# The order of three VectorE steps in the last stage of a one-core encoder block

## The chip, the cores and the metric

The kernel runs on one NeuronCore of a Trainium2 chip. The metric is the device time of one execution in microseconds (us). The times given are medians of several runs; the profile is that of one further execution.

## The reference, cut to what matters

The block is an attention mixer followed by a product-key expert layer. All the work around the change lies in the expert layer, whose experts are single neurons chosen per token. For 256 tokens of width 2048 and 16384 experts:

```python
def block_fn(args):
    tb, ib, gb = args
    u = expert_u[ib]
    a = jax.nn.gelu(jnp.einsum('thkd,td->thk', u, tb), approximate=False)
    vv = expert_v[ib]
    return jnp.einsum('thk,thkd->td', (gb * a).astype(vv.dtype), vv)
...
x = x + peer_ffn(h, peer_wq, peer_keys, peer_u, peer_v)
return rms_norm(x, norm_final_g)
```

The kernel computes the first 214 tokens densely: the products with all rows of `peer_u` (stage "u"), the gelu and the gates, and then the products with all rows of `peer_v` (stage "down"). The other 42 tokens are computed by gathering just the rows that their gates chose, three copies of 42 tokens side by side (126 partitions).

## The kernel before, in words

Each stage streams its weights in **chunks** of 128 x 1024 float32 (512 KB). To multiply in float32 accuracy, each operand is split into a high half (a rounded copy in the type fp32r) and a low half (the rest). A chunk passes through these engines:

- SP issues its load into one of four `raw` buffers (`load`, line 474). It first waits on `lo_ready`, until the low half of the chunk four earlier is made, since that is the last reader of the buffer.
- ScalarE copies `raw` to `hi` (`hi_of`, line 637) and, in the down stage, makes the high half of the chunk's activations in one of four `act_now` buffers (`act_hi_of`, line 956).
- VectorE makes the activations' low half (`act_lo_of`, line 1564; it waits for that chunk's `act_hi_of`) and the weights' low half (`lo_of`, line 1047; it waits for `hi` and, through `low_used`, until TensorE is done with the chunk two earlier, since there are two `lo` buffers).
- TensorE multiplies: eight products of `hi` with both halves of the activations (line 1962, the "highs"), and eight of `lo` with the high half (line 1966, the "lows"). Even chunks do highs and then lows, odd chunks lows and then highs. So the lows of an even chunk and of the odd one behind it stand next to each other, and TensorE needs the two `lo` tiles shortly after one another.

The down stage has 256 chunks, numbered here from 0, in two halves of 128 (output columns 0 to 1023, then 1024 to 2047). `BODY` is 4: the loops do four chunks a round, `s` is the place in the round.

Between chunks VectorE has a second job, the **row work** for the 42 gathered tokens. In chunks 2, 4, ..., 36 of the stage there is a dot product of a gathered row (`dots_at`, line 1486), then two small steps on the weights (`weights_at`), and then 43 row additions in each half (`rows_at`, lines 1599 and 1602). In the first half the additions come in nearly every second chunk, in the second half in nearly every third. GpSimd issues the gathers for this work (line 599) into three `rows` buffers; each waits for the row work that frees its buffer.

All orders are written out by hand and each engine executes its own in sequence. The VectorE function `down` is what the change touches.

Of the kernel before, what the change touches and what calls it, by code (L numbers as in the profile page):

```python
# [37 lines left out]
BODY = 4  # L38
# [93 lines left out]
HALF = CHUNKS["down"] // BODY // 2  # L132
# [128 lines left out]
def build(nc, A, out):  # L261
    with ExitStack() as ctx:
# [199 lines left out]
        def pick1(t, i):  # L462
            return flat(t[:, bass.ds(i, 1), :])
# [575 lines left out]
        def _(v):  # L1039
# [3 lines left out]
            def lo_of(cb, it, s):  # L1043

                v.wait_ge(hi_ready, it * BODY + cb + s + 1)
                v.wait_ge(low_used, it * BODY + cb + s - LOS + 1 + RAW)
                nc.vector.tensor_tensor(lo[s % LOS][:], raw[s % RAW][:], hi[s % RAW][:].bitcast(F32), ALU.subtract  # L1047
                                        ).then_inc(lo_ready, 1)
# [440 lines left out]
            def dots_at(it, s):  # L1489
                for n in dots_of(it, s):  # L1490
                    dot_of(n)
# [69 lines left out]
            def act_lo_of(it, s, j):  # L1561

                v.wait_ge(act_hi_ready, it * BODY + (s + 1))
                nc.vector.tensor_tensor(act_now[s % ACTS][:, TD:2 * TD], pick1(act, j), act_now[s % ACTS][:, 0:TD].bitcast(F32),  # L1564
                                        ALU.subtract).then_inc(act_lo_ready, 1)
# [15 lines left out]
            def weights_at(it, s):  # L1581
                if (it, s) == (WEIGHED, 1):
                    v.wait_ge(dot_done, STEPS)
                    nc.vector.tensor_tensor(w_s, dots[0:NP, 0:PICKS], dots[0:NP, PICKS:STEPS], ALU.add).then_inc(w_summed, 1)
                if (it, s) == (WEIGHED + 1, 1):
                    v.wait_ge(w_gelu, 1)
                    v.wait_ge(idx_ready, 1)
                    nc.vector.tensor_tensor(w_s, w_s, gates_s[0:NP, :], ALU.mult).then_inc(w_ready, 1)

            def rows_at(it, s, half):  # L1590
                for m in adds_of((it - HALF * half) * BODY + s, half):
                    n = half * PICKS + m
                    own = acc[0:NP, half * CW:(half + 1) * CW]
                    g = STEPS + n
                    row = rows[g % ROWS][0:NP, :]
                    v.wait_ge(row_landed[g % ROWS], 16 * (g // ROWS + 1))
                    if m == 0:
                        v.wait_ge(w_ready, 1)
                        nc.vector.tensor_scalar(own, row, w_s[:, 0:1], None, ALU.mult).then_inc(row_added, 1)
                    else:  # L1600
                        v.wait_ge(row_added, n)
                        nc.vector.scalar_tensor_tensor(out=own, in0=row, scalar=w_s[:, m:m + 1], in1=own,  # L1602
                                                       op0=ALU.mult, op1=ALU.add).then_inc(row_added, 1)

            def down(it, half, last=False):
                for s in range(BODY):
                    if not (last and s == 3):
                        if it not in (0, HALF) or s:
                            act_lo_of(it, s + 1, (it - HALF * half) * BODY + s + 1)
                        lo_of(CHUNK0["down"], it, s + 1)  # L1610
                    if half == 0:
                        dots_at(CHUNKS["u"] // BODY + it, s)
                    weights_at(it, s)
                    rows_at(it, s, half)
                    fold_squares(it, s)

            def fold_squares(it, s):

                if it == FOLDED and s in (0, 1, 2):
                    n = 4 >> s  # L1620
                    v.wait_ge(x2_sq, 2)
                    if s:
                        v.wait_ge(sq_folded, s)
                    nc.vector.tensor_tensor(sq2[:, 0:n, :], sq2[:, 0:n, :], sq2[:, n:2 * n, :], ALU.add).then_inc(sq_folded, 1)
# [16 lines left out]
            for it in range(HALF):  # L1641
                down(it, 0, last=it == HALF - 1)
# [5 lines left out]
            for it in range(HALF, 2 * HALF):  # L1648
                down(it, 1, last=it == 2 * HALF - 1)
# [500 lines left out]
```

## Time and profile before

| | |
|---|---|
| median of 3 runs | 2113.71 us (2113.15 to 2114.25) |
| profiled execution, own time | 2119.6 us |
| its span, first to last instruction | 2117.8 us |
| granted TensorE clock, mean | 0.996 of full speed |
| TensorE busy (share of the span) | 2084.9 us (98%) |
| TensorE weight loads | 1979.6 us (93%) |
| VectorE | 1618.2 us (76%) |
| ScalarE | 1178.6 us (56%) |
| GpSimd | 415.6 us (20%) |

The profiled execution took 5.9 us more than the median of the runs, and its span lies 1.8 us inside its own time. Busy time of TensorE includes pipelined matmuls whose ends are modelled, so 98% does not say that nothing was waited for; the gaps between its weight loads tell that better. The down stage begins at about 1453 us of the span and its last product starts at 2102 us.

### The profile page before, as it was taken

What the parts mean: (1) busy time and instruction counts of PE and PEld (TensorE: products, weight loads), DVE (VectorE), ACT (ScalarE), POOL (GpSimd) and SP (SyncE); (2) the same over time, 40 slices, a digit from 0 to 9 for tenths busy, and PEclk for the clock granted to TensorE, in tenths of its full rate; (3) what the DMA queues carried; (4) which work ended last, traced back from release to release, by engine and by line L of the source; (5) the groups of instructions that cost most, each with busy time, mean ns of one, the idle gap of its engine ahead of it and who ended that gap; (6) DMA issues with size and microseconds to landing.
All of it is one profiled execution on the core that took longest, in us unless ns stands there. A gap on an engine that the chain in (4) does not pass through costs nothing.

```text
span 2117.8 us, 41324 instructions
## 1 busy us (share of the span) xinstructions
PE 2084.9 (98%) x13482; PEld 1979.6 (93%) x13482; DVE 1618.2 (76%) x2678; ACT 1178.6 (56%) x2082; POOL 415.6 (20%) x306
## 2 busy tenths in 40 slices
PE   8999999999999999999999999999999999999997
PEld 6888888889989999999999999999999999999997
DVE  6555566666766986888788999888878887777776
ACT  5444455445555555555877777555554554555554
POOL 0000000000000000000766775333313321121110
PEclk9999999999999999999999999999999999999998
DMA  7655554445557456666777777999989897888883
GB/s 244 235 193 185 184 168 158 159 139 191 182 185 249 153 172 215 213 213 229 256 250 249 246 252 241 317 323 323 338 294 314 307 336 264 284 280 294 279 296 136
DMA packets 141088, 505.50 MB, mean 239 GB/s; under 512 B 16158, under 2 KB 19102, under 8 KB 140630
## 3 DMA queue, kind: packets, MB, share of 16 engines
q1 hardware_dynamic: 116072, 414.42, 57.9%
q0 software_dynamic: 24768, 90.19, 12.2%
q8 instruction: 28, 0.46, 0.1%
q14 instruction: 46, 0.38, 0.1%
q10 hardware_dynamic: 174, 0.05, 0.0%
HBM read 500.36 MB, written 4.24 MB: 238 GB/s over the span
## 4 chain that ended last, share of the span: by engine, by line
PE 89%; DVE 5%; DMA 3%; issue 2%; ACT 0%; DVEq 0%; SPq 0%; ACTq 0%
PE ps L1679 35%; PE ps L1686 19%; PE ps L1962 15%; PE ps L1966 9%; PE ps L1708 5%; DMA raw<-w_down 3%; PE ps L1944 2%; DVE lo L1047 2%; PE ps L1805 1%; PE ps L1787 1%; PE ps L1796 0%; DMA x_t<-x_t 0%; DVE acc L1602 0%; DVE score_b L1355 0%; DVE idx_now L1357 0%
## 5 line engine op out<-in xcount | busy, mean ns | idle before, releaser
L1047 DVE TENSOR_TENSOR lo<-raw,hi 128x1024 fp32r<-128x1024 f32 x760 | 925.3, 1225 | 307.4 <-PE ps L1686 200.2
L637 ACT CAST hi<-raw 128x1024 fp32r<-128x1024 f32 x760 | 791.5, 1047 | 366.0 <-DMA raw<-w_down 282.3
L1679 PE MATMUL ps<-move_u,hi 128*128 128x428 f32 x2048 | 435.2, 360 | 0.0
L1962 PE MATMUL ps<-act_now,hi 128*128 128x428 f32 x2048 | 429.2, 360 | 1.8 <-DVE x L1628 1.4
L1962 PEld LDWEIGHTS ps<-act_now,hi 128*128 128x128 f32 x2048 | 377.6, 190 | 15.3 <-DVE x L1628 2.5
L1679 PE MATMUL ps<-move,hi 128*128 128x512 f32 x1536 | 379.4, 396 | 10.1 <-ACT hi L637 10.1
L1679 PEld LDWEIGHTS ps<-move_u,hi 128*128 128x128 f32 x2048 | 371.8, 189 | 10.8
L1679 PEld LDWEIGHTS ps<-move,hi 128*128 128x128 f32 x1536 | 281.6, 189 | 63.5 <-issue 10.1
L645 ACT COPY upper<-ps 128x214 f32<-128x214 f32 (+1 forms) x224 | 78.9, 352 | 438.3 <-PE ps L1679 438.0
L1966 PEld LDWEIGHTS ps<-act_now,lo 128*128 128x128 f32 x2048 | 253.2, 192 | 8.8 <-issue 5.8
L1966 PE MATMUL ps<-act_now,lo 128*128 128x214 f32 x2048 | 255.0, 275 | 4.7 <-DVE lo L1047 3.6
L1686 PEld LDWEIGHTS ps<-move_u,lo 128*128 128x128 f32 x2048 | 248.4, 191 | 3.9 <-DVE lo L1047 1.8
L1686 PE MATMUL ps<-move_u,lo 128*128 128x214 f32 x2048 | 248.4, 274 | 1.5 <-DVE lo L1047 1.5
L1686 PEld LDWEIGHTS ps<-move,lo 128*128 128x128 f32 x1536 | 198.1, 191 | 11.2 <-DVE move L1099 1.3
L599 POOL DMA_INDIRECT rows<-u_rows,idx x86 | 114.2, 1328 | 461.4 <-ACT gates_s L878 314.2
L1686 PE MATMUL ps<-move,lo 128*128 128x256 f32 x1536 | 202.3, 284 | 1.0 <-DVE move L1272 0.9
L599 POOL DMA_INDIRECT rows<-w_down,idx x86 | 120.1, 1397 | 413.5 <-DVE acc L1602 356.8
L617 POOL TENSOR_SCALAR one_j<-iota,j_t,gate_t 128x128 f32<-128x128 f32 x107 | 170.1, 1590 | 89.2 <-PE ps L1944 85.6
L1564 DVE TENSOR_TENSOR act_now<-act,act_now 128x214 fp32r<-128x214 f32 x256 | 96.3, 376 | 57.1 <-ACT act_now L956 56.6
L1602 DVE SCALAR_TENSOR_TENSOR acc<-rows,dots,acc 126x1024 f32<-126x1024 f32 x84 | 107.4, 1279 | 1.2 <-DMA rows<-w_down,idx 1.2
L1486 DVE CUSTOM_DVE_ANT_0 rows<-rows,h_rows 126x1024 f32<-126x1024 f32 x86 | 104.7, 1218 | 0.0
L1708 PE MATMUL ps<-move,hi 128*128 128x256 f32 x512 | 97.4, 287 | 2.6 <-DVE lo L1047 2.4
(210 smaller groups left out, 1660.2 us busy)
## 6 DMA issues: line engine op xcount, KB each, us to landing
raw<-w_u SPq DMA_DIRECT2D x256, 512.0 KB, 4.3
raw<-w_down SPq DMA_DIRECT2D x256, 512.0 KB, 5.9
raw<-w_qk SPq DMA_DIRECT2D x68, 512.0 KB, 4.3
raw<-w_gate SPq DMA_DIRECT2D x64, 512.0 KB, 3.4
raw<-w_out SPq DMA_DIRECT2D x32, 512.0 KB, 3.8
raw<-w_pq SPq DMA_DIRECT2D x32, 512.0 KB, 3.3
raw<-w_v SPq DMA_DIRECT2D x28, 512.0 KB, 4.4
raw<-w_o SPq DMA_DIRECT2D x24, 512.0 KB, 3.5
```

The costliest lines, as they stand in the source:

```text
L599: nc.gpsimd.indirect_dma_start(rows[g % ROWS][:], None, lines, bass.IndirectOffsetOnAxis(ap=idx[:, n:n + 1], axis=0)).then_inc(row_landed[ ...
L617: nc.gpsimd.tensor_scalar(one_j[n % 4][:, 0, :], iota128[:], j_t[:, 2 * n:2 * n + 1], gate_t[:, 2 * n:2 * n + 1], ALU.is_equal, ALU.mult). ...
L637: nc.scalar.copy(hi[slot][:], raw[slot][:]).then_inc(hi_ready, 1)
L1047: nc.vector.tensor_tensor(lo[s % LOS][:], raw[s % RAW][:], hi[s % RAW][:].bitcast(F32), ALU.subtract).then_inc(lo_ready, 1)
L1486: nc.vector.tensor_tensor_reduce(row, row, h_rows[0:NP, c:c + CW], 1.0, 0.0, ALU.mult, ALU.add, dots[0:NP, n:n + 1]).then_inc(dot_done, 1)
L1564: nc.vector.tensor_tensor(act_now[s % ACTS][:, TD:2 * TD], pick1(act, j), act_now[s % ACTS][:, 0:TD].bitcast(F32), ALU.subtract).then_inc( ...
L1602: nc.vector.scalar_tensor_tensor(out=own, in0=row, scalar=w_s[:, m:m + 1], in1=own, op0=ALU.mult, op1=ALU.add).then_inc(row_added, 1)
L1679: ins = nc.tensor.matmul(ps[bank][:, 0:2 * w], hi[slot][:, col:col + P], m, start=begins, stop=ends)
L1686: ins = nc.tensor.matmul(ps[bank][:, 0:w], lo[lslot][:, col:col + P], m[:, 0:w], start=False, stop=False, skip_group_check=True)
L1708: ins = nc.tensor.matmul(ps[bank][:, 0:T], w[:, col:col + P], x, start=begins, stop=ends)
L1962: return nc.tensor.matmul(ps[d][:, 0:2 * TD], hi[s % RAW][:, d * P:(d + 1) * P], act_now[s % ACTS][:], start=begins, stop=ends)
L1966: return nc.tensor.matmul(ps[d][:, 0:TD], lo[s % LOS][:, d * P:(d + 1) * P], act_now[s % ACTS][:, 0:TD], start=False, stop=False, skip_gro ...
```

## The change

In each chunk's step of the down stage, `lo_of` of the next chunk now comes first, and then `act_lo_of` of the chunk after that one, where before `act_lo_of` and `lo_of` of the next chunk stood together in that order. The first two activations of each half are made ahead of the loops in both versions.

```diff
             def down(it, half, last=False):
                 for s in range(BODY):
                     if not (last and s == 3):
-                        if it not in (0, HALF) or s:
-                            act_lo_of(it, s + 1, (it - HALF * half) * BODY + s + 1)
                         lo_of(CHUNK0["down"], it, s + 1)
+                    if not (last and s >= 2):
+                        act_lo_of(it, s + 2, (it - HALF * half) * BODY + s + 2)
                     if half == 0:
                         dots_at(CHUNKS["u"] // BODY + it, s)
                     weights_at(it, s)
```

What this does to VectorE's sequence is seen in the built programs. First a place in the first half with a row addition between an even chunk (`lo0`) and the odd one behind it (`lo1`); `act_now1` is the odd chunk's activations. Before:

```order
L1564 TENSOR_TENSOR act_now0_84<-act_145,act_now0_84 128x214
L1047 TENSOR_TENSOR lo0_57<-raw0_49,hi0_53 128x1024
L1602 SCALAR_TENSOR_TENSOR acc_153<-rows2_152,dots_155,acc_153 126x1024
L1564 TENSOR_TENSOR act_now1_85<-act_145,act_now1_85 128x214
L1047 TENSOR_TENSOR lo1_58<-raw1_50,hi1_54 128x1024
```

The same place on VectorE after the change:

```order
L1564 TENSOR_TENSOR act_now0_84<-act_145,act_now0_84 128x214
L1047 TENSOR_TENSOR lo0_57<-raw0_49,hi0_53 128x1024
L1564 TENSOR_TENSOR act_now1_85<-act_145,act_now1_85 128x214
L1602 SCALAR_TENSOR_TENSOR acc_153<-rows2_152,dots_155,acc_153 126x1024
L1047 TENSOR_TENSOR lo1_58<-raw1_50,hi1_54 128x1024
```

The row addition has moved past one instruction: from ahead of the odd chunk's `act_now` to behind it, directly ahead of that chunk's `lo`. The tiles' sequence without the row work is the same. The second place is in the stage's first chunks, where the row work is a dot product (two instructions). Before, on VectorE:

```order
L1047 TENSOR_TENSOR lo0_57<-raw0_49,hi0_53 128x1024
L1486 ISA rows2_152,dots_155<-rows2_152,h_rows_147 126x1024
L1486 ISA dots_155 126x1
L1564 TENSOR_TENSOR act_now1_85<-act_145,act_now1_85 128x214
L1047 TENSOR_TENSOR lo1_58<-raw1_50,hi1_54 128x1024
```

And after the change:

```order
L1047 TENSOR_TENSOR lo0_57<-raw0_49,hi0_53 128x1024
L1564 TENSOR_TENSOR act_now1_85<-act_145,act_now1_85 128x214
L1486 ISA rows2_152,dots_155<-rows2_152,h_rows_147 126x1024
L1486 ISA dots_155 126x1
L1047 TENSOR_TENSOR lo1_58<-raw1_50,hi1_54 128x1024
```

Again the row work and `act_now` have changed places. Chunks with no row work between them show no difference, and the programs of TensorE, ScalarE, GpSimd and SP are the same in both versions.

## Rows read from the trace of the kernel before

**Rows 1.** Busy time by stretch: first half, then second half of the down stage.

```profile
core 0: us, PE busy (x) PEld busy (x) DVE busy (x) ACT busy (x) POOL busy (x), PEclk, DMA share, GB/s
1461.00:1766.00 305.00, 300.78 (x1941) 293.01 (x1941) 251.26 (x324) 158.96 (x246) 88.73 (x60) 1.00 0.90 319
1790.00:2090.00 300.00, 299.53 (x1948) 292.79 (x1946) 232.25 (x288) 164.72 (x255) 52.56 (x40) 1.00 0.82 280
```

**Rows 2.** The chain of work that ended last: start us, us, what.

```profile
1719.21 3.14 PE ps L1962 x16
1722.35 1.78 PE ps L1966 x16
1724.13 3.14 PE ps L1962 x16
```

**Rows 3.** TensorE's weight loads: lows of chunk 6, and of chunk 124.

```profile
1470.58 1.95 PEld L1966 LDWEIGHTS ps<-act_now,lo 128*128 128x128 f32 x16
...
1766.59 1.06 PEld L1966 LDWEIGHTS ps<-act_now,lo 128*128 128x128 f32 x8
```

**Rows 4.** Waits, 1461 to 1766 us: us in total, times, longest.

```profile
ACT hi L637 <- DMA raw<-w_down: 140.0, 73, 4.9
...
DVE act_now L1564 <- ACT act_now L956: 26.8, 32, 2.8
DVE lo L1047 <- PE ps L1966: 24.3, 32, 2.1
```

**Rows 5.** VectorE in order of time around chunks 56 and 57.

```profile
1591.37 1.23 DVE L1047 TENSOR_TENSOR lo<-raw,hi 128x1024 fp32r<-128x1024 f32 x1 [0.74 <-PE ps L1966]
1592.51 1.28 DVE L1602 SCALAR_TENSOR_TENSOR acc<-rows,dots,acc 126x1024 f32<-126x1024 f32 x1
1594.66 0.38 DVE L1564 TENSOR_TENSOR act_now<-act,act_now 128x214 fp32r<-128x214 f32 x1 [0.87 <-ACT act_now L956]
1594.96 1.22 DVE L1047 TENSOR_TENSOR lo<-raw,hi 128x1024 fp32r<-128x1024 f32 x1
1596.10 0.37 DVE L1564 TENSOR_TENSOR act_now<-act,act_now 128x214 fp32r<-128x214 f32 x1
```

**Rows 6.** SP's issues of the loads of chunks 57 and 61.

```profile
1585.80 0.33 SPq L474 DMA_DIRECT2D raw<-w_down  x1
...
1596.35 0.33 SPq L474 DMA_DIRECT2D raw<-w_down  x1
```

**Rows 7.** ScalarE's copies of chunks 57, 61 and 132, started by their loads' landing.

```profile
1593.31 1.05 ACT L637 CAST hi<-raw 128x1024 fp32r<-128x1024 f32 x1 [3.38 <-DMA raw<-w_down]
...
1601.76 1.05 ACT L637 CAST hi<-raw 128x1024 fp32r<-128x1024 f32 x1 [1.21 <-DMA raw<-w_down]
...
1786.19 1.05 ACT L637 CAST hi<-raw 128x1024 fp32r<-128x1024 f32 x1 [6.99 <-DMA raw<-w_down]
```

**Rows 8.** VectorE, first and last of the meetings counted in the prediction.

```profile
1468.15 1.22 DVE L1486 CUSTOM_DVE_ANT_0 rows<-rows,h_rows 126x1024 f32<-126x1024 f32 x1
...
1469.87 0.38 DVE L1564 TENSOR_TENSOR act_now<-act,act_now 128x214 fp32r<-128x214 f32 x1 [0.49 <-ACT act_now L956]
...
1759.25 1.28 DVE L1602 SCALAR_TENSOR_TENSOR acc<-rows,dots,acc 126x1024 f32<-126x1024 f32 x1
1760.71 0.38 DVE L1564 TENSOR_TENSOR act_now<-act,act_now 128x214 fp32r<-128x214 f32 x1 [0.18 <-ACT act_now L956]
```

**Rows 9.** Loads, median us to landing: 1461 to 1770 us, then 1790 to 2090 us.

```profile
raw<-w_down SPq DMA_DIRECT2D x124, 512.0 KB, 6.7
...
raw<-w_down SPq DMA_DIRECT2D x119, 512.0 KB, 5.0
```

**Rows 10.** GpSimd's gathers next to the loads of chunks 57 and 61.

```profile
1584.79 1.65 POOL L599 DMA_INDIRECT rows<-w_down,idx  x1 [3.98 <-DVE acc L1602]
...
1594.56 0.94 POOL L599 DMA_INDIRECT rows<-w_down,idx  x1 [3.41 <-DVE acc L1602]
```

**Rows 11.** The load of chunk 132, issued after a pause.

```profile
1782.79 0.33 SPq L474 DMA_DIRECT2D raw<-w_down  x1
```

**Rows 12.** VectorE in the second half: chunks 158 and 159.

```profile
1851.87 1.23 DVE L1047 TENSOR_TENSOR lo<-raw,hi 128x1024 fp32r<-128x1024 f32 x1 [0.78 <-PE ps L1966]
1855.34 0.38 DVE L1564 TENSOR_TENSOR act_now<-act,act_now 128x214 fp32r<-128x214 f32 x1 [2.24 <-ACT act_now L956]
1855.64 1.22 DVE L1047 TENSOR_TENSOR lo<-raw,hi 128x1024 fp32r<-128x1024 f32 x1
1856.78 1.28 DVE L1602 SCALAR_TENSOR_TENSOR acc<-rows,dots,acc 126x1024 f32<-126x1024 f32 x1
```

## The prediction, made before the changed kernel was run

> **What bounds the kernel now.** I looked first at busy time by stretch, since the change touches the down stage alone. In both halves TensorE's row is full (300.78 of 305 us, 299.53 of 300) at the full clock, 1.00 [rows 1]. The chain of waits then gives TensorE's own pace: from one run of 16 highs to the next is 1724.13 - 1719.21 = 4.92 us for a pair of chunks [rows 2]. The gaps between weight loads tell how near the stage is to that pace. From the lows of chunk 6 to those of chunk 124 lie 59 pairs, so 290.3 us at 4.92; the trace has 1766.59 - 1470.58 = 296.0 [rows 3]. TensorE waited 5.7 us there, 5.02 us a pair.
>
> What it waits for is seen in the list of waits. ScalarE waits 140.0 us for landing weights in the first half, and VectorE 26.8 us, 32 times, for ScalarE's activations, which ScalarE makes right behind that landing [rows 4]. So loads are late by a little, and VectorE stands behind them. It is not late everywhere: as many times, 32, its `lo` waits for TensorE to free a buffer [rows 4].
>
> **The ring.** A load goes out when VectorE has made the `lo` four chunks earlier. Chunk 57 shows the whole round: its load is issued at 1585.80 and that of chunk 61 at 1596.35, so 10.55 us [rows 6]. Of these, 7.51 pass until ScalarE starts on the landed chunk at 1593.31 [rows 7], and 3.04 from there to the next issue (copy, activations, `act_now`, `lo`, issue). Four chunks, two pairs, take TensorE 9.84 us. With the median landing of the first half, 6.7 us [rows 9], a round is 6.7 + 3.04 = 9.74 us: it just fits. That the loads are at the edge is what makes the change dear or free.
>
> **What the change does.** It removes no instruction and adds none; no duration changes. Only the row work moves, 18 dot products and 86 row additions in the stage and five small steps, each past one `act_now` instruction. That instruction waits for ScalarE, and so for the next load. Two cases:
>
> Where the activations are already there, the row work starts 0.30 us later (the spacing of `act_now` and the next instruction, 1594.96 - 1594.66 [rows 5]) and `lo` starts when it did. The cover is VectorE's own sequence; the gather behind the row work goes out 0.30 us later, three buffers ahead of its use. Cost 0. TensorE gets its activations up to 1.20 us sooner, and had not been waiting for them. Gain 0.
>
> Where they are not yet there, row work used to fill the wait. At chunk 57 it starts at 1592.51, and `act_now` can start only at 1594.66 [rows 5]. The moved row addition would start at 1594.96 and push `lo` to 1596.16. One addition takes 1.20 us to the next start (1.28 us long, overlapping by 0.08); a dot product about 1.14 with its read-out. What is queued behind: `lo` of the odd chunk, TensorE's lows, which wait for it, and the load of chunk 61, which goes out 1.20 us later as well. Nothing hides that where the `lo` belongs to an odd chunk, since TensorE wants it right after the even one.
>
> **How often.** I compared, for each row work of the stage, its start with the end of the activations that it now has to wait for. In the first half 47 of 63 start before that end, the first at 1468.15, the last at 1759.25, where `act_now` follows at 1469.87 and 1760.71 [rows 8]. Thirty-four of them sit between an even and an odd chunk: 16 dot products and 18 additions. In the second half only two do. The reason is the spacing. The load that lands late is the one whose gather goes out right behind it: the gather of chunk 52's row ends its issue at 1584.79 + 1.65 = 1586.44, 0.64 us behind load 57, which took 7.51 us [rows 6, 7, 10]; load 61, with a gather 0.85 ahead (1594.56 + 0.94), took 5.41 [rows 6, 7, 10]. Row work of chunk c thus delays the load of chunk c + 5, and with row work in every second chunk the one of chunk c + 4 stands just ahead of it. With every third chunk it does not: at the late chunk 159 `act_now` waits 2.24 us, and the row addition comes only behind that chunk's `lo` [rows 12]. I take 0 for the second half.
>
> **The sum.** Taken one by one, with all else as it was, the first half's meetings delay the `lo` tiles by 45 us, and where TensorE has less slack than that it stalls 19.6 us in all: 17.5 of it at odd chunks, 2.1 at four even ones, whose lows come after eight more highs. But one stall makes the next smaller, unless the loads go out later too. So I go by the ring. A colliding pair's round becomes landing + 3.04 + 1.17 (between 1.14 and 1.20), against 9.84.
>
> - If landing stays at 6.7 us, the round is 10.91 and a pair takes 5.455 us, 0.535 above TensorE's pace.
> - If landing shortens as the pair stretches, I read its slope from the two halves: 6.7 us at 319 GB/s, 5.0 at 280 [rows 1, 9]. At 5.20 us a pair the same bytes need 319 x 5.02 / 5.20 = 308 GB/s, on that line a landing of 6.2, and a round of 10.41, which is 5.20 a pair. So 0.28 above.
>
> The second half's transfers are fewer and otherwise spaced, so the slope flatters; and every moved row has its gather right behind the load. Against it, a later load finds less ahead of it. I take the middle, 0.41 us for each of 34 pairs: 13.9 us. Those pairs' share of the 5.7 us already waited for, 34 of 59 or 3.3 us, is inside it and goes off; the even chunks add 2.1. **Sum +12.7 us.** The profiled execution took 2119.6 us and would take 2132.3; it lies 5.9 above the median of the runs, so the median goes from 2113.7 to 2126.4 us. By the two ends of the landing it is +8.3 (0.28 x 34 - 3.3 + 2.1) and +17.0 (0.535 x 34, likewise).
>
> **The rivals.**
>
> *The delay is hidden (2115.7 us).* If the DMA engines have a backlog, a load issued 1.2 us later lands when it would have. Then landing falls by what the issue loses: with load 61's 5.41 us the round is 5.41 + 3.04 + 1.17 = 9.62, under 9.84, and only the first collision of each run of them costs. There are four runs (from chunks 6, 50, 82 and 112) at up to 1.1 us each, since TensorE, once late, is no longer caught; I take half, +2. For it: the DMA engines are 90% busy in the first half [rows 1]. Against it: the quick loads are those without a gather on top, and the moved order keeps the gather there. It decides if landings at odd chunks drop below 9.84 - 4.21 = 5.63 us.
>
> *Landings grow (about 2139 us).* The load of chunk 132, with nothing beside it, took 1786.19 - 1782.79 = 3.40 us [rows 7, 11], and load 57 with a gather on top more than twice that, 7.51. If sharing with the gather is what makes a load long, a longer pair does not shorten it. Halfway between the median and that load, at 7.1, the round is 11.31, 0.735 above the pace, and the sum 25.0 - 3.3 + 2.1 = +23.8. The Trainium skill's page "DMA: Bandwidth & Descriptors", section "Queues, rings and completion order", says that each DMA engine takes turns between the queue rows that have work, a packet at a time. By that rule a load beside a gather gets half of the engine however long the pair is, which is this rival and not the slope; the two rows agree with it in size, 3.40 against 7.51, but do not separate it from the backlog of other loads.
>
> *Faster (2108.0 us).* The row work goes later, and so does its gather. If that moves gathers away from the load that now suffers, landings at odd chunks fall from 7.51 towards 5.41, and the 5.7 us of waiting in the first half go: 2113.7 - 5.7. It decides if gathers end their issue well over 1 us behind the load or ahead of it. Against it: the load follows `lo`, `lo` directly follows the row work, and the gather follows the same row work, so the two stay together.
>
> **How the numbers follow.** The forecast (ring slowed, +5 to +19) gets 0.50, longer landings 0.16, hidden 0.26, faster 0.08. A difference of 0.2%, 4.2 us, is about what a measurement can tell from no change here; the runs of before lie within 1.1 us. Slower by more takes the forecast and the longer landings, 0.66; the hidden case is within it, with a little of the faster one, 0.27; 0.07 remains for faster. The range reaches from under the hidden case to where the longer landings begin to end, 2115 to 2138 us; the forecast's own is 2119 to 2133.
>
> **What would show it.** In the first half VectorE's waits for ScalarE's activations rise from 26.8 us by up to 45, as row work no longer fills them; its waits for TensorE's lows fall from 24.3. Row additions stand directly ahead of `lo` with no wait between. The 59 pairs from chunk 6 to chunk 124 take 308 to 310 us in place of 296.0, and TensorE's waits are for `lo` of odd chunks. The second half keeps its pace within 1 us, busy times stay the same, and everything before 1453 us too. Wrong would be: the waits moved as said, and the 59 pairs near 296 (landings shortened); or odd loads quicker than in before; or the second half losing as well, which would mean that its spacing does not protect it.

## The result

The changed kernel took 2129.29 us (median of 6 runs, 2123.02 to 2136.67) against 2113.86 us for the kernel before (6 runs, 2113.15 to 2114.89): a ratio of 1.0068 with a 95% interval of 1.0056 to 1.0081, so +15.4 us. The forecast was +12.7. (The ratios given here and below are not the quotients of the medians shown, here 1.0073, and differ from them by up to 0.001.) What was not forecast at all is the spread: 13.7 us between the runs, where before had 1.7 beside it. In the later groups, of 21 to 29 runs, before itself spread over 7.1 to 10.3 us, so most of that spread may not be the change's.

### The profile page after: what moved, and what is told of

Its sections match the earlier page's. It is cut to its first block, busy times and chain, and to the rows that moved or that the text cites. A ratio compares the mean times of both kernels' runs of the same rounds, so it can differ in the third digit from the quotient of the medians.

```text
span 2128.2 us, 41324 instructions
## 1 busy us (share of the span) xinstructions
PE 2084.9 (98%) x13482; PEld 1978.7 (93%) x13482; DVE 1617.8 (76%) x2678; ACT 1178.0 (55%) x2082; POOL 408.8 (19%) x306
## 3 DMA queue, kind: packets, MB, share of 16 engines
HBM read 500.36 MB, written 4.24 MB: 237 GB/s over the span
## 4 chain that ended last, share of the span: by engine, by line
PE 82%; DMA 7%; DVE 7%; issue 2%; ACT 1%; SPq 0%; ACTq 0%; DVEq 0%
PE ps L1679 35%; PE ps L1686 19%; PE ps L1962 11%; DMA raw<-w_down 7%; PE ps L1966 6%; PE ps L1708 5%; DVE lo L1047 3%; PE ps L1944 2%; DVE acc L1602 1%; PE ps L1787 1%; PE ps L1805 1%; DVE rows L1486 0%; PE ps L1796 0%; ACT act_now L956 0%; DVE act_now L1564 0%
## 5 line engine op out<-in xcount | busy, mean ns | idle before, releaser
L1966 PEld LDWEIGHTS ps<-act_now,lo 128*128 128x128 f32 x2048 | 253.4, 192 | 21.8 <-issue 18.6
L599 POOL DMA_INDIRECT rows<-w_down,idx x86 | 112.5, 1309 | 427.9 <-DVE acc L1602 371.7
L1564 DVE TENSOR_TENSOR act_now<-act,act_now 128x214 fp32r<-128x214 f32 x256 | 96.4, 376 | 84.6 <-ACT act_now L956 83.7
```

The lines of the kernel that those rows point to most:

```text
L599: nc.gpsimd.indirect_dma_start(rows[g % ROWS][:], None, lines, bass.IndirectOffsetOnAxis(ap=idx[:, n:n + 1], axis=0)).then_inc(row_landed[ ...
L1966: return nc.tensor.matmul(ps[d][:, 0:TD], lo[s % LOS][:, d * P:(d + 1) * P], act_now[s % ACTS][:, 0:TD], start=False, stop=False, skip_gro ...
```

## The profile after the change

The profiled execution took 2129.97 us, 0.7 above the median. By stretch (the two halves of the down stage, as in [rows 1]):

```profile
core 0: us, PE busy (x) PEld busy (x) DVE busy (x) ACT busy (x) POOL busy (x), PEclk, DMA share, GB/s
1461.00:1766.00 305.00, 291.51 (x1864) 282.75 (x1865) 239.71 (x311) 152.48 (x234) 81.56 (x58) 0.99 0.87 305
1790.00:2090.00 300.00, 297.52 (x1921) 289.35 (x1920) 232.91 (x294) 160.94 (x252) 51.93 (x40) 1.00 0.82 280
```

The first half fell from 300.78 us of TensorE's work to 291.51 in the same 305 us, at the same clock within a hundredth; the second half gave up 2 us. TensorE's weight loads, lows of chunk 6 and of chunk 124, which answer to [rows 3]:

```profile
1470.14 1.06 PEld L1966 LDWEIGHTS ps<-act_now,lo 128*128 128x128 f32 x8
...
1779.04 1.05 PEld L1966 LDWEIGHTS ps<-act_now,lo 128*128 128x128 f32 x8
```

These 59 pairs took 1779.04 - 1470.14 = 308.9 us where before had 296.0: +12.9. The waits from 1461 to 1776 us, where [rows 4] has 1461 to 1766 (columns: us in total, times, longest):

```profile
ACT hi L637 <- DMA raw<-w_down: 144.0, 82, 4.5
...
DVE act_now L1564 <- ACT act_now L956: 38.9, 31, 2.8
DVE lo L1047 <- PE ps L1966: 27.5, 31, 2.4
...
PE ps L1966 <- DVE lo L1047: 13.9, 16, 1.8
```

VectorE's waits for activations rose by 12.1 us with about as many of them (31 for 32), and TensorE now waits 13.9 us, in 16 pieces of up to 1.8, for `lo`. One such place is chunk 85. First VectorE in order of time (start, us, what, in brackets the idle time before and its releaser):

```profile
1669.50 1.22 DVE L1047 TENSOR_TENSOR lo<-raw,hi 128x1024 fp32r<-128x1024 f32 x1
1673.23 0.38 DVE L1564 TENSOR_TENSOR act_now<-act,act_now 128x214 fp32r<-128x214 f32 x1 [2.50 <-ACT act_now L956]
1673.53 1.28 DVE L1602 SCALAR_TENSOR_TENSOR acc<-rows,dots,acc 126x1024 f32<-126x1024 f32 x1
1674.72 1.22 DVE L1047 TENSOR_TENSOR lo<-raw,hi 128x1024 fp32r<-128x1024 f32 x1
```

Then TensorE's weight loads at the same place, and SP's issues of the loads of chunks 85 and 89:

```profile
1673.23 1.05 PEld L1966 LDWEIGHTS ps<-act_now,lo 128*128 128x128 f32 x8
1676.06 0.97 PEld L1966 LDWEIGHTS ps<-act_now,lo 128*128 128x128 f32 x8 [1.78 <-issue]
```

```profile
1664.27 0.33 SPq L474 DMA_DIRECT2D raw<-w_down  x1
...
1676.11 0.33 SPq L474 DMA_DIRECT2D raw<-w_down  x1
```

VectorE stood idle for 2.50 us, made the activations at 1673.23, then the row addition, which waited for nothing, and only at 1674.72 the odd chunk's `lo`. TensorE had finished the even chunk's lows and waited 1.78 us. The next load of that buffer went out at 1676.11, a round of 11.84 us; that of chunk 57 in before was 10.55 [rows 6]. At chunk 56 of before the same idle time was filled by the row addition [rows 5].

Loads in the first half landed after a median of 5.8 us (6.7 before), those of the second half after 5.9 (5.0 before), in the stretches of [rows 9]:

```profile
raw<-w_down SPq DMA_DIRECT2D x119, 512.0 KB, 5.8
...
raw<-w_down SPq DMA_DIRECT2D x121, 512.0 KB, 5.9
```

## The experiments

Each kernel was timed beside the kernel before on the same chip; before had medians of 2114.1, 2113.0 and 2114.8 us in the three groups. "The stretch" below is always chunk 6 to chunk 124, 59 pairs, 290.3 us at TensorE's pace, of the one profiled execution. All diffs are against the changed kernel, and those of `down` show the lines that make and place the activations.

**Which half.** `first_half` has the changed order in the first half alone, `second_half` in the second alone.

```diff
-                    if not (last and s >= 2):
+                    if not (half == 1) and not (last and s >= 2):
                         act_lo_of(it, s + 2, (it - HALF * half) * BODY + s + 2)
...
                     rows_at(it, s, half)
+                    if half == 1 and not (last and s >= 2):
+                        act_lo_of(it, s + 2, (it - HALF * half) * BODY + s + 2)
```

In `second_half` the two conditions have `half == 0`.

> The changed order in the first half of the down stage alone, the order of before in the second. Theory (row work behind the activations' wait delays the lo of odd chunks, which happens in the first half only): the whole loss is here, 2126 to 2130 us, and the 118 chunks from chunk 6 to chunk 124 take 306 to 311 us. Rival one (the second half loses too, since its waits for activations also rose, 25.5 to 41.6 us): 2121 to 2125 us. Rival two (the loss is not tied to a place): about half of it, 2121 us, and the sum of this run's and the next one's losses is not 15 us.

> The order of before in the first half, the changed order in the second alone. Theory: 2113 to 2115 us, as before. Rival one: 2116 to 2121 us, with TensorE waiting for lo of odd chunks in the second half; the profile of the changed kernel has 2.2 us more there than that of before.

Measured: `first_half` 2130.41 us, ratio 1.0069 (1.0056 to 1.0083); `second_half` 2114.77 us, ratio 1.0001 (0.9991 to 1.0010). The whole loss belongs to the first half. The 2.2 us that the second half of the changed kernel's profile had over that of before are not in the medians. The stretch of `first_half`'s profile, 304.3 us, lies under the 306 to 311 expected, though its median lies at the upper end of what was expected: one profile tells the size of the loss less well than the medians do.

**Which row work.** `dots_only` moves only the dot products, `adds_only` only the first half's additions.

```diff
-                    if not (last and s >= 2):
+                    if half == 0 and it <= 8 and not (last and s >= 2):
                         act_lo_of(it, s + 2, (it - HALF * half) * BODY + s + 2)
...
                     rows_at(it, s, half)
+                    if not (half == 0 and it <= 8) and not (last and s >= 2):
+                        act_lo_of(it, s + 2, (it - HALF * half) * BODY + s + 2)
```

That is `dots_only`, whose last dot product stands in round 8; `adds_only` has `it >= 9` in both places.

> Only the 18 dot products of the stage's first 36 chunks stand behind the activations; all row additions stand ahead of them as before. Theory: 16 of the 34 delayed odd chunks are here. At the even rate of the sum (0.41 us a pair) that is 16/34 of the loss, about 7 us: 2120 to 2121 us; by the profile of the changed kernel, which lost 8.3 us by chunk 37, it is 2122 us. Rival (what is lost early starts a backlog that costs all the way): 2126 us or more. If dot products cost nothing, 2114 us.

> The complement of dots_only: only the first half's row additions (from chunk 38 on) stand behind the activations; dot products and second half as before. If the two parts add up to first_half (16.3 us, of which dots_only had 5.5): 2122 to 2126 us. By the profile of the changed kernel, which lost 4.6 us from chunk 38 to 124: 2118 to 2119 us. If late loads from the dot products were needed to start the additions' bad rounds: 2114 us, as before.

Measured: `dots_only` 2119.58 us, 1.0021 (1.0008 to 1.0034), +5.5; `adds_only` 2125.06 us, 1.0054 (1.0036 to 1.0072), +10.2. They add up to 15.7, against 16.3 for `first_half` and 15.4 for the change. So, as far as intervals of some 3 and 4 us can tell, losses are local: what the dot products lose early starts nothing that costs later. The profile of the changed kernel, with 4.6 us from chunk 38 on against that of before (221.1 and 216.5), understated the additions; against `second_half`, which has the order of before there and took 213.1, it is 8.0.

**Which chunks.** In four kernels all row work of the stage stands on one side: `even_*` between the `lo` of an even chunk and that of the odd one behind it, `odd_*` one chunk further on, each in the order of before and in the changed one.

```diff
-DOT_AT = [it * BODY + s for it in range(UR, (CHUNKS["u"] + CHUNKS["down"]) // BODY) for s in (1, 3)
+DOT_AT = [it * BODY + s for it in range(UR, (CHUNKS["u"] + CHUNKS["down"]) // BODY)
+          for s in ((1, 3) if it < CHUNKS["u"] // BODY else (0, 2))
...
-    return tuple(m for m in range(PICKS) if first + int(m * apart) == c)
+    if half:
+        return tuple(m for m in range(PICKS) if 2 + 2 * int(m * 1.44) == c)
+    return tuple(m for m in range(PICKS) if (40 + 2 * m if m else 41) == c)
```

That is `odd_after`; `even_after` leaves `DOT_AT` alone and has `3 + 2 * int(m * 1.44)` and `41 + 2 * m`. In `odd_before` and `even_before` the activations stand behind `rows_at`, as in the order of before.

> The changed order, with all row work of the stage moved by one chunk, so that it stands between the lo of an odd chunk and the lo of the even one behind it, still behind the activations' wait. Theory one (the cost comes from TensorE wanting the lo of an odd chunk right behind that of the even one, while ahead of an even chunk it has sixteen more products to do): little loss or none, 2110 to 2117 us. Theory two (the ring alone: landing + 3.04 + 1.17 us against 9.84, which holds for the buffers of even chunks as for those of odd ones; the slack ahead of an even chunk is used up after two or three rounds): as much as the change or more, 2126 to 2135 us.

> The order of before, with all row work of the stage moved by one chunk, so that it stands between an odd chunk's lo and the activations of the even chunk behind it. Against odd_after it differs in the changed steps' order alone. Ring theory (row work behind the activations' wait makes a buffer's round longer at either kind of chunk): the order of before gets back what odd_after lost, 2109 to 2115 us. Rival (odd_after lost because of where the gathers went, not because of the wait ahead of the row work): about 2122 us here too.

> The changed order, with all row work between the lo of an even chunk and that of the odd one behind it: in the first half 59 such pairs with the dot products, where the changed kernel has 34. Theory (each such pair loses about the same): 15 us x 59/34 = 26 us, 2136 to 2144 us, and some more in the second half. Rival (only the dot products and a few runs of bad rounds cost; additions in step with the chunks settle into quick landings): 2122 to 2130 us.

> The order of before, with all row work between the lo of an even chunk and that of the odd one behind it; odd_before (2106.7 us) had it one chunk on. Theory (TensorE has 0.89 us between the lows of an even and an odd chunk and 3.1 us of other products ahead of the next even one, so the place matters in the order of before too): 2114 to 2120 us. Rival (odd_before gained because row work at every second chunk is regular, where that of before drifts from even to odd chunks and back): 2105 to 2109 us.

| row work stands | order of before | changed order |
|---|---|---|
| mixed (the two kernels of this study) | 2113.86 us, stretch 296.0 | 2129.29 us, 1.0068, stretch 308.9 |
| ahead of odd chunks' `lo` (even) | 2120.51 us, 1.0027 (1.0017 to 1.0037), stretch 294.3 | 2148.99 us, 1.0152 (1.0134 to 1.0170), stretch 312.9 |
| ahead of even chunks' `lo` (odd) | 2106.72 us, 0.9962 (0.9949 to 0.9975), stretch 290.6 | 2122.47 us, 1.0030 (1.0018 to 1.0043), stretch 299.8 |

The stretch of `odd_before` and of `even_after`, first and last row of each:

```profile
1469.20 1.40 PEld L1971 LDWEIGHTS ps<-act_now,lo 128*128 128x128 f32 x11
...
1759.76 1.06 PEld L1971 LDWEIGHTS ps<-act_now,lo 128*128 128x128 f32 x8
```

```profile
1470.46 1.40 PEld L1968 LDWEIGHTS ps<-act_now,lo 128*128 128x128 f32 x11
...
1783.37 1.05 PEld L1968 LDWEIGHTS ps<-act_now,lo 128*128 128x128 f32 x8
```

The changed order loses in every row of the table (by the ratios 0.68% mixed, 1.25% even, 0.68% odd), most ahead of odd chunks, but ahead of even chunks as well: `odd_after` fell between its two theories. The ring's rounds do get longer at even chunks too: over the 57 even chunks of the stretch with row work ahead of them, worked out from both traces, the mean round is 9.83 us in `odd_before` and 10.18 in `odd_after`. That TensorE's slack there takes up the rest of the delay is argued and not shown. `even_after` lost more than the 26 us of its theory, since its second half loses as well, and by place even `even_before` is dearer than before. `odd_before` was quicker than its theory's 2109 to 2115. The waits of `odd_after` from 1461 to 1776 us:

```profile
ACT hi L640 <- DMA raw<-w_down: 148.8, 85, 4.2
...
DVE act_now L1567 <- ACT act_now L959: 55.5, 42, 3.4
```

and those of `odd_before`:

```profile
ACT hi L640 <- DMA raw<-w_down: 130.8, 69, 3.9
...
DVE act_now L1567 <- ACT act_now L959: 17.1, 22, 1.9
```

The same row work at the same places, and the wait for activations is 55.5 us where it can't be filled and 17.1 where it can. `odd_before` runs the stretch in 290.56 us, TensorE's own pace to within 0.3 us, and is faster than both kernels of this study.

**How much row work.** `half_rows` keeps the changed order and halves what is pushed.

```diff
+                w = CW // 2 if n >= STEPS - 18 else CW
+                row = row[:, 0:w]
-                nc.vector.tensor_tensor_reduce(row, row, h_rows[0:NP, c:c + CW], 1.0, 0.0, ALU.mult, ALU.add,
+                nc.vector.tensor_tensor_reduce(row, row, h_rows[0:NP, c:c + w], 1.0, 0.0, ALU.mult, ALU.add,
...
-                    own = acc[0:NP, half * CW:(half + 1) * CW]
+                    w = CW // 2 if m else CW
+                    own = acc[0:NP, half * CW:half * CW + w]
...
```

> The changed order; the stage's dot products and row additions work on half a row (512 of 1024 elements; part of the computation is left out), the gathers and waits are as they were. Ring theory: what is pushed past the wait is about 0.62 us and not 1.17, so a round is 5.8 (the landing that the changed kernel shows) + 3.04 + 0.62 = 9.46, under 9.84, or with 6.7 of before 10.36, 0.26 a pair too long: 2113 to 2122 us, the loss cut by half at least. Rival (the loss does not hang on the length of the row work but on where its gather goes out): 2126 us or more.

Measured: 2115.10 us (2105.31 to 2122.84 over 12 runs), 1.0003 (0.9989 to 1.0017). Half the work brings back nearly all of the loss. That would fit a limit better than a price per instruction, but it is not shown: shorter row work also eases the rest of VectorE's sequence, and the order of before with half the row work was not run. This run alone would not settle the cause. Its runs spread over 17.5 us.

**The gathers.** `no_gather` is the changed kernel without the 86 gathers for the additions, `no_gather_b` the kernel before without them.

```diff
-            for n in range(STEPS):
-                gather("w_down", n)
...
-                    v.wait_ge(row_landed[g % ROWS], 16 * (g // ROWS + 1))
```

> The changed order with the 86 gathers for the row additions left out; the additions stay, on what the buffers hold (part of the computation is left out). The dot products keep their gathers. Ring theory: with nothing beside them loads land in 3.4 to 4 us, a round is at most 4 + 3.04 + 1.17 = 8.2 us against 9.84, so the order costs nothing from chunk 38 on: 43 pairs to chunk 124 take 211.6 to 213 us where the changed kernel took 221.1, and only the some 8 us of the dot products stay: 2112 to 2117 us, 7 to 9 above no_gather_b. Rival (VectorE's push stalls TensorE whatever the landing): chunk 38 to 124 stays at 217 us or more.

> The order of before with the same 86 gathers left out. Ring theory: 2104 to 2109 us, since the waits of before from chunk 38 on go as well (216.2 us there in the profile of before, 211.6 at TensorE's pace). Rival (the gathers do not lengthen the loads): 2113 to 2114 us, as before.

Measured: 2113.93 us (2109.06 to 2116.99) and 2106.76 us (2105.50 to 2111.59), ratios 1.0001 (0.9992 to 1.0011) and 0.9966 (0.9953 to 0.9979). The two are 7.2 us apart. Chunks 38 and 124 of `no_gather`:

```profile
1553.57 1.40 PEld L1963 LDWEIGHTS ps<-act_now,lo 128*128 128x128 f32 x11
...
1765.12 1.06 PEld L1963 LDWEIGHTS ps<-act_now,lo 128*128 128x128 f32 x8
```

and its loads from 1461 to 1770 us:

```profile
raw<-w_down SPq DMA_DIRECT2D x124, 512.0 KB, 3.5
```

With these gathers gone, a load lands in a median of 3.5 us, the activations are there when VectorE comes, and these 43 pairs take 211.55 us, TensorE's pace to within 0.1 us, with the changed order and all row additions in place. So the cost takes both: row work behind the wait, and a wait to stand behind. Of the 7.2 us that stay, the dot products, whose gathers were left in, account for most: chunks 6 to 38 took 83.7 us in the profile of `no_gather` and 78.7 in that of `no_gather_b`, 5.0 more (5.5 in the medians of `dots_only`). No row shows the rest.

**The wait itself.** `act_early` keeps the changed order, the row work's places, the loads and the gathers, but ScalarE makes each chunk's high activations before it waits for the load of the chunk ahead of that one (at the start of each half, for chunk 2 as well, in lines left out here).

```diff
                 for s in range(BODY):
...
+                    if not (last and s >= 1):
+                        act_free(it, s + 3)
+                        act_hi_of(it, s + 3, (it - HALF * half) * BODY + s + 3)
                     if not (last and s >= 2):
                         hi_of(CHUNK0["down"], it, s + 2)
-                        if isinstance(it, int) and it == 0 and s == 0:
-                            a.wait_ge(chunk_used, CHUNK0["down"] + RAW)
-                        else:
-                            act_free(it, s + 2)
-                        act_hi_of(it, s + 2, (it - HALF * half) * BODY + s + 2)
```

> The changed order; ScalarE makes the high half of each chunk's activations ahead of the landing of the load of the chunk before it, so that act_lo never stands behind a late load. The row work stays behind act_lo, and the loads, gathers and sizes are as they were. Theory (the cost is that row work can no longer fill VectorE's wait for the load): nearly all of the loss goes, 2106 to 2116 us, and VectorE's waits are for hi and for TensorE, with act_now near 0. Rival (the cost is not in this wait, but in the gathers' place or in the row work's nearness to lo): 2124 us or more.

Measured: 2109.82 us (2106.03 to 2114.60), 0.9977 (0.9965 to 0.9989), stretch 290.28 us, TensorE's pace:

```profile
1470.79 1.39 PEld L1970 LDWEIGHTS ps<-act_now,lo 128*128 128x128 f32 x11
...
1761.08 1.06 PEld L1970 LDWEIGHTS ps<-act_now,lo 128*128 128x128 f32 x8
```

Its waits from 1461 to 1776 us:

```profile
DVE lo L1051 <- PE ps L1970: 44.1, 56, 1.9
...
DVE lo L1051 <- ACT hi L637: 6.0, 9, 1.1
DVE act_now L1568 <- ACT act_now L956: 4.3, 1, 4.3
```

and VectorE around chunk 85, the place shown of the changed kernel:

```profile
1660.25 0.38 DVE L1568 TENSOR_TENSOR act_now<-act,act_now 128x214 fp32r<-128x214 f32 x1
1660.54 1.28 DVE L1606 SCALAR_TENSOR_TENSOR acc<-rows,dots,acc 126x1024 f32<-126x1024 f32 x1
1662.11 1.23 DVE L1051 TENSOR_TENSOR lo<-raw,hi 128x1024 fp32r<-128x1024 f32 x1 [0.29 <-ACT hi L637]
```

with ScalarE's copy of that chunk, which begins when the load has landed:

```profile
1661.03 1.05 ACT L637 CAST hi<-raw 128x1024 fp32r<-128x1024 f32 x1 [1.47 <-DMA raw<-w_down]
```

Here too `hi` waits for the load, until 1661.03, but `act_lo` no longer stands behind it (1660.25), the row addition fills the time, and `lo` comes 1.08 us after the landing. In the changed kernel that copy began at 1671.88, so there it was 1674.72 - 1671.88 = 2.84:

```profile
1671.88 1.05 ACT L637 CAST hi<-raw 128x1024 fp32r<-128x1024 f32 x1 [4.18 <-DMA raw<-w_down]
```

The loads of `act_early` are not quicker, a median of 6.5 us in the first half. The loss is gone with the wait. The edit does one thing more: it takes the activations out of the way from a landed load to the next issue, which shortens that way for every chunk. The order of before with the same edit was not run, so how much of the gain below before comes from this is open; but a stretch at TensorE's pace leaves no room for a cost of the changed order.

## Why the prediction held, point by point

- **Only row work moves, and it costs where VectorE waits for activations.** Shown by the two pairs `odd_*` and `even_*`, which differ in the order alone, by `act_early`, which takes away that wait, and by `no_gather`, which takes away the late loads.
- **First half yes, second half 0.** Shown for the sizes by `first_half` and `second_half`. The reason given, the spacing of nearly three chunks, is only partly borne out: `even_after`, whose second half has the same number of additions but some of them two chunks apart, takes 308.6 us from chunk 132 to chunk 252 against 296.7 in `even_before`. The second half is not immune.
- **The ring, landing + 3.04 + 1.17.** The step that carried the sum. Over the 41 odd chunks of the stretch with row work ahead of them, worked out row by row from both traces, the median time from ScalarE's start on the landed chunk to the next issue for its buffer grew from 3.22 us to 4.24; the terms had said 3.04 and 4.21. The median landing of those loads fell from 6.82 to 6.43 us, so the round became 10.67 us against TensorE's 9.84. The way to the next issue thus grew by 1.02 us where the term said 1.17. The starting point was off: at these places before had 6.82 + 3.22 = 10.04, so the ring did not "just fit" (9.74) there. And 6.43 lies in the middle of the forecast's two landings (6.2 and 6.7) by luck, being the middle of two kinds: 15 of the 41 loads took under 5.63 us, where before had 8, and most of the rest 6 to 8.
- **0.41 us for each of 34 pairs, and 2.1 for the even chunks.** The prices can now be had from the table: `even_after` less `even_before` is 18.6 us for 57 places, 0.33 each; `odd_after` less `odd_before` is 9.2 us for some 56, 0.16 each. The changed kernel has row work at 41 places of the first kind in the stretch and 17 of the second: 41 x 0.33 + 17 x 0.16 = 16.3 us, and its profile shows 12.9. The forecast's 13.9 + 2.1 - 3.3 has the same size (13.9 - 3.3 is 0.31 for each of its 34), but the loss isn't spread evenly: TensorE lost it in 16 waits of up to 1.8 us, all of them ahead of an odd chunk's lows, while other rounds lost nothing.
- **From the profile to the median.** Forecast +12.7, in the stretch of the profiles +12.9, of the medians +15.4. What was mis-sized is the offset: the profiled execution of before took 5.9 us more than its median and I carried that over, but that of the changed kernel lies only 0.7 above. The stretch of `second_half`, which has before's order there and a profiled execution at its median, took 293.0 us, so the 5.7 us of waiting that I subtracted a share of (3.3) may be more than the usual run has. That is one profile, so it is argued and not shown.
- **Waits for activations up by as much as 45 us.** They rose by 12.1. The 45 was the sum with all else as it was, and the prediction said that one stall makes the next smaller; 14 us came back as TensorE's own waits. Two more signs came out otherwise than said: VectorE's waits for TensorE's lows, which were to fall from 24.3 us, are 27.5, and odd loads quicker than in before, named as a sign of being wrong, were found (6.43 for 6.82), too little quicker to hide the cost.
- **Why a load is late.** This step failed. "The load that lands late is the one whose gather goes out right behind it" does not hold in the changed kernel: load 57 goes out at 1592.83, its gather ends its issue 0.64 us behind it, as in [rows 10], and yet the load is there after 3.50 us and not 7.51:

```profile
1592.29 1.18 POOL L599 DMA_INDIRECT rows<-w_down,idx  x1 [3.75 <-DVE acc L1602]
```

```profile
1592.83 0.33 SPq L474 DMA_DIRECT2D raw<-w_down  x1
```

```profile
1596.33 1.05 ACT L637 CAST hi<-raw 128x1024 fp32r<-128x1024 f32 x1 [1.18 <-DMA raw<-w_down]
```

Gathers do make loads late on the whole (3.5 us without them), but not by their place behind a load alone. That place does not even sort the loads: of the 41 it is 0.64 us at 24 in before and at 33 in the changed kernel, quick loads and long ones. What sets the two loads 57 apart is what the DMA queues moved from issue to ScalarE's start (packets, MB, share of the engines; q1 has the loads, q0 the gathers). In before, 1585.80 to 1593.31:

```profile
q1 hardware_dynamic: 436, 1.57, 67.1%
q0 software_dynamic: 148, 0.54, 17.9%
```

and in the changed kernel, 1592.83 to 1596.33:

```profile
q1 hardware_dynamic: 191, 0.65, 57.6%
q0 software_dynamic: 77, 0.32, 22.5%
```

The rate is about the same, 2.11 MB in 7.51 us and 0.97 in 3.50, some 280 GB/s. Load 57 itself is 0.52 MB of it, so 1.05 MB of other chunks' loads passed during its way in before and 0.13 in the changed kernel: they, more than the gathers' 0.54 and 0.32, make the difference. Whether they went ahead of it or beside it is not shown. The slope of landing against GB/s falls as well: `odd_before` has 5.1 us at 325 GB/s, where the forecast's line had 6.7 at 319 and 5.0 at 280.

The Trainium skill's page "DMA: Bandwidth & Descriptors", section "Queues, rings and completion order", says that each DMA engine takes turns between the queue rows that it has work for; worked out from that, an estimate for a load with a gather beside it all the way is about twice the 3.40 us of one alone. Load 57 of the changed kernel does not test it: in the first 2.52 us of its way (1592.83 to 1595.35) only the load queue moved anything. Load 57 of before matched it in size by luck: one gather is 0.52 MB (126 rows of 4 KB), or 1.8 us at 281 GB/s, and would make 5.2 us of 3.40 and not 7.51.

- **The rivals.** "Hidden" asked for landings under 5.63 us at the odd chunks; the median was 6.43. "Landings grow" asked for 7.1. "Faster" asked for gathers to move away from the loads; they kept their place. All three fall for the change as made, but "hidden" holds for a part of the rounds: from the lows of chunk 46 to those of chunk 62, with row work pushed ahead of a `lo` in every pair and landings of 3.4 to 4.6 us at the odd chunks, the changed kernel's eight pairs took 39.36 us, TensorE's pace.

```profile
1577.61 1.18 PEld L1966 LDWEIGHTS ps<-act_now,lo 128*128 128x128 f32 x9
...
1616.97 1.06 PEld L1966 LDWEIGHTS ps<-act_now,lo 128*128 128x128 f32 x8
```

The 5.7 us of waiting that the faster rival hoped for were there to be had, by another way: `odd_before` with the row work moved by a chunk (ratio 0.9962) and `act_early` (0.9977) both beat the two kernels of this study. They were not put together.

What stays open: why rounds fall into quick or long landings, and how much of the changed kernel's spread of 13.7 us comes from that. Its granted clock does not follow the time (0.996 in the run of 2123.02 us, 0.997 in that of 2136.67). That small shifts send rounds one way or the other, as at chunk 57, would do it; no run here separates that.

## What to carry to other kernels

On an engine that runs in order, independent work directly ahead of an instruction that waits fills its wait; moved behind it, it delays what follows by up to its full length where the wait is real (1.19 us at chunk 85), although nothing was added. On average it cost less, 0.33 us a place in the stretch of the `even_*` kernels. Before such a move, count how often the wait ends last, and look whether the buffer that the delayed instruction frees is in a ring that just fits. If the waiting instruction can be fed from something other than the late load, as ScalarE's activations were in `act_early`, the cost of the order can go: there the stretch ran at TensorE's pace.

## What the hardware did that I had not expected

After TensorE's wait of 1.92 us between weight loads, which ended at 1505.46 in the changed kernel, its granted clock was lower for a while. The windows, and the 16 weight loads that follow:

```profile
1500.00:1505.00 5.00, 3.72 (x23) 3.45 (x21) 2.46 (x5) 2.64 (x4) 0.52 (x1) 1.00 0.93 317
1505.00:1510.00 5.00, 4.51 (x19) 4.29 (x20) 4.73 (x8) 3.37 (x5) 2.47 (x2) 0.68 0.79 268
1510.00:1515.00 5.00, 5.00 (x33) 4.89 (x33) 2.73 (x5) 1.91 (x4) 0.37 (x1) 0.98 0.91 317
```

```profile
1506.35 4.57 PEld L1962 LDWEIGHTS ps<-act_now,hi 128*128 128x128 f32 x16
```

A mean of 0.68 is partly the upper level (2.4 GHz) and partly the lower one (1.2 GHz). The run of 16 highs took 4.57 us and not 3.14 [rows 2], so this wait cost 1.4 us more than itself. The wait of 1.78 us at chunk 85 brought no such fall. At the end of the kernel the two profiles differ in the same way: over the last products the granted clock was 0.77 in before (2096 to 2103 us) and 1.00 in the changed kernel (2107 to 2114 us), which gives the changed profile back some 2 us. Whether the timed runs differ in this way no trace shows.
